# Three projection passes of each attention round moved from slots 12, 14 and 19 to slots 23, 24 and 25

## The reference

```python
proj = n @ w_in[l]                                   # n = RMSNorm(h)
qa, ka, va, qb, kb, vb, gate_a, gate_b = jnp.split(proj, split_at, axis=-1)
o_a = merge(_dilated_attention(qa, ka, heads(va)))   # 8 heads of 64, softmax
o_b = merge(_stick_breaking(qb, kb, vb))             # 8 heads of 64, strictly causal
mixed = (jax.nn.sigmoid(gate_a) * (o_a @ w_up_a[l])
         + jax.nn.sigmoid(gate_b) * (o_b @ w_up_b[l]))
h = h + mixed @ w_out[l]
```

## Time and profile before

| | |
|---|---|
| Median of 3 runs | 1794.56 us (1794.41 to 1795.36) |
| Profiled execution | 1795.2 us, span 1793.3 us |
| TensorE busy | 1709.0 us, 95% of the span |
| VectorE, ScalarE, GpSimd busy | 1145.5, 794.0, 767.5 us |
| TensorE's mean granted clock | 0.991 of full |
| Round 1, first logits (279.88) to those of round 2 (458.21) | 178.3 us |

### The profile page before, as it was taken

The page is one execution under the profiler, slowest core; times in us unless marked ns, Lnnn a source line. Parts: engine busy times, 40 slices in busy tenths (PEclk is TensorE's granted clock), DMA queues, the critical chain, the costliest instruction groups (busy, mean ns, idle before and its releaser), DMA issues.

```text
span 1793.3 us, 24747 instructions
## 1 busy us (share of the span) xinstructions
PE 1709.0 (95%) x8354; PEld 1382.6 (77%) x8354; DVE 1145.5 (64%) x1677; ACT 794.0 (44%) x1304; POOL 767.5 (43%) x876
## 2 busy tenths in 40 slices
PE   5799999999999999999999997999999999999997
PEld 4677777787777777777887875788888888788885
DVE  7536884688468955976644789554554455566665
ACT  6335773577357746863312445443333334100013
POOL 3552322232223221334554334666566566444446
PEclk9899999999999999999999998999999999999999
DMA  5231012102111211245312001222223222422222
GB/s 203 65 118 49 29 54 67 48 29 66 64 39 33 72 56 42 99 157 200 112 47 94 24 24 35 71 71 94 70 70 102 85 70 74 161 94 94 94 94 94
DMA packets 51717, 141.80 MB, mean 79 GB/s; under 512 B 6193, under 2 KB 14641, under 8 KB 51505
## 3 DMA queue, kind: packets, MB, share of 16 engines
q1 hardware_dynamic: 32400, 101.62, 16.4%
q10 hardware_dynamic: 19232, 39.07, 6.7%
HBM read 109.20 MB, written 30.41 MB: 78 GB/s over the span
## 4 chain that ended last, share of the span: by engine, by line
PE 78%; DVE 8%; issue 4%; POOL 2%; ACT 2%; POOLq 0%; DVEq 0%; ACTq 0%
PE ps L569 44%; PE ps L950 22%; PE ps L686 4%; PE ps L649 3%; PE ps L663 3%; DVE e_row L1792 1%; DVE e_row L1789 1%; POOL w_lo L519 1%; DVE rows L1801 1%; DVE pt L1825 1%; DVE sum_a L2019 1%; PE ps L682 1%; PE ps L901 0%; DVE n_lo L2025 0%; PE ps L878 0%
## 5 line engine op out<-in xcount | busy, mean ns | idle before, releaser
L480 POOL TENSOR_SCALAR w_hi<-w_stage 128x512 fp32r<-128x512 f32 x164 | 108.8, 682 | 773.2 <-issue 393.6
L569 PE MATMUL ps<-n_hi,w_hi 128*128 128x512 f32 x1120 | 307.9, 396 | 5.5 <-DVE n_lo L1737 1.9
L485 POOL TENSOR_TENSOR w_lo<-w_stage,w_hi 128x256 fp32r<-128x256 f32 x328 | 301.9, 952 | 6.8
L569 PE MATMUL ps<-n_hi,w_lo 128*128 128x512 f32 x1120 | 303.7, 392 | 0.0
L569 PE MATMUL ps<-n_lo,w_hi 128*128 128x512 f32 x1120 | 303.1, 392 | 0.0
L569 PEld LDWEIGHTS ps<-n_hi,w_hi 128*128 128x128 f32 x1120 | 206.5, 188 | 50.6 <-issue 3.5
L569 PEld LDWEIGHTS ps<-n_lo,w_hi 128*128 128x128 f32 x1120 | 207.9, 188 | 42.6 <-issue 0.2
L569 PEld LDWEIGHTS ps<-n_hi,w_lo 128*128 128x128 f32 x1120 | 207.9, 188 | 42.3
L519 POOL TENSOR_TENSOR w_lo<-w_stage,w_hi 128x256 fp32r<-128x256 f32 x176 | 165.1, 959 | 120.5 <-ACT w_hi L1423 120.2
L1913 DVE TENSOR_TENSOR h<-ps,h 128x512 f32<-128x512 f32 (+1 forms) x176 | 121.3, 690 | 122.3 <-PE ps L569 121.9
L1208 ACT ACTIVATE pt<-ps 128x256 fp32r<-128x256 f32 (+3 forms) x96 | 78.0, 813 | 132.9 <-PE ps L663 132.9
(11 more groups left out here) (260 smaller groups left out, 3179.2 us busy)
## 6 DMA issues: line engine op xcount, KB each, us to landing
w_stage<-weights_in SPq DMA_DIRECT2D x116, 512.0 KB, 3.5
w_stage<-weights_in SPq DMA_DIRECT2D x44, 256.0 KB, 2.9
hidden_scratch<-u_f SPq DMA_DIRECT2D x22, 512.0 KB, 5.4
n_lo<-hidden_scratch SPq DMA_DIRECT2D x22, 512.0 KB, 4.1
gates_scratch<-raw ACTq DMA_DIRECT2D x16, 512.0 KB, 3.0
o_scratch<-o_sum ACTq DMA_DIRECT2D x64, 64.0 KB, 2.2
g_b<-gates_scratch ACTq DMA_DIRECT2D x8, 512.0 KB, 4.2
h<-x_t_in ACTq DMA_DIRECT2D x8, 512.0 KB, 9.2
```

What stands on the lines that cost most here:

```text
L480: ins = pool.tensor_scalar(w_hi[:, b, at], stage[:, b, at], 1.0, 1.0, ALU.mult, ALU.mult)
L485: ins = pool.tensor_tensor(w_lo[:, b, at], stage[:, b, at], w_hi[:, b, at].bitcast(F32), ALU.subtract)
L569: ins = pe.matmul(bank, w[:, b, c:c + P], mv(k), start=(first and n == 0), stop=(last and n == total - 1))
```

## The change

The list of passes per slot of `ROUND` is written anew. The first twelve slots keep their numbers. Before, slots 12 to 27 had 3, 2, 3, 2, 3, 2, 2, 3, 2, 1, 1, 1, 1, 1, 1, 2 passes; now they have 2, 2, 2, 2, 3, 2, 2, 2, 2, 1, 1, 2, 2, 2, 1, 2. The tiles keep their order, so every pass from VA's third on is dealt out one to three places later. `LAST` is as it was.

```diff
 ROUND = Plan(("KB", "QB", "QA", "KA", "VB", "VA", "G0", "G1", "G2", "G3"),
-             [3] * 6 + [2] * 6 + [3, 2, 3, 2, 3, 2, 2, 3, 2] + [1] * 6 + [2], {"TB": (12, 14), "TA": (18, 20)})
+             [3] * 6 + [2] * 6 + [2, 2, 2, 2, 3, 2, 2, 2, 2, 1, 1, 2, 2, 2, 1, 2], {"TB": (12, 14), "TA": (18, 20)})
```

## The result

| | before | after |
|---|---|---|
| Median | 1794.96 us (1794.41 to 1795.68, 4 runs) | 1806.63 us (1804.02 to 1809.54, 4 runs) |
| Profiled execution, span | 1795.2, 1793.3 us | 1804.02, 1802.2 us |
| Round 0, first logits to first logits | 178.83 us | 181.56 us |
| Round 1 | 178.33 us | 180.33 us |
| Round 2 | 176.45 us | 180.98 us |

The change is slower by 11.7 us; the ratio to before is 1.0067, 95% interval 1.0051 to 1.0083. The forecast was 1807.5 us, range 1801 to 1813. The profiled execution is the fastest of the four and 2.6 us under their median, so the traces explain +8.8 us of the 11.7. Rounds 0 to 2 are 9.3 us longer, and the rest of the execution 0.5 us shorter.

What follows compares the result with a forecast made beforehand. TensorE and VectorE were taken to be in balance in slots 12 to 22, TensorE to set the tail. Tail 4.0 + 4.0 + 3.4, removals 3 x 0.3, clock 0.8: +13.1 us on 1794.56, say 1807.5; range 1801 to 1813 us.

Steps and rivals of the forecast that it cites:

- The removals give nothing: Slots 12, 14 and 19: passes taken out become TensorE waits or lateness, with no gain.
- Slot 14's wait: Ahead of slot 14's `attend`: TensorE's wait grows from 0.91 to 2.84 us, taking up slot 12's removed pass.
- the net of slots 12 to 22 is +0.3 us a round: Slots 12 to 22: the three removals together cost +0.3 us a round, bounds -1.3 and +1.0.
- the lateness of slot 16's `attend`: Slot 16: a later `pt` starts `attend` at about 390.5 instead of 390.06; TensorE carries 0.4 us to slot 19's logits.
- fall beside other VectorE work: Slots 12 to 22: reads and GpSimd's weight splits at new times; if they fall badly, +1.0 us a round.
- The tail: Slots 23 to 25: three added passes cost 5.7 us less waits behind them: +4.0, +4.0, +3.4 us in rounds 0 to 2.
- The clock: Low granted clock behind longer waits, mattering in slot 16 and round 2's slot 23: half a stretch, +0.8 us.
- rival 3: Low clock behind each new wait, slot 16 in three rounds and round 2's slot 23: +6.3 us, 1813 us; chance 0.14.
- That the waits are filled (1): VectorE is not the bound; slots 12, 14 and 19 shorten by 5.7 us a round: 1789.5 us; chance 0.05.
- That slot 19's wait goes away (2): VectorE's 1.60 us wait for chunk 19's softplus vanishes: -1.3 instead of +0.3 each round, 1802 us; chance 0.12.
- That nothing comes of it (4): Whole kernel: the work is the same and the time stays at 1794.6 us; chance 0.04.
- The sum: Whole kernel: 4.0 + 4.0 + 3.4 + 3 x 0.3 + 0.8 = +13.1 us, about 1807.5 us.

Runs made afterwards that it cites:

- The experiment without the nine passes: Kernel before with one projection pass left out in each of slots 12, 14 and 19 of rounds 0 to 2: 1795.56 us against 1795.22.
- The read moved by itself: Kernel before with only VectorE's read of VA's first half moved from slot 13 to slot 14, rounds 0 to 2: 1796.56 us against 1796.05.
- the experiment with nine passes more: Kernel before with one more projection pass in each of slots 23, 24 and 25 of rounds 0 to 2: 1808.51 us against 1795.22.
- no longer of the second: Kernel before with two passes moved, from slots 10 and 11 to 22 and 23 (1795.72 us) or 22 and 24 (1796.54 us), against 1795.93.
- the single moves: Kernel before with one pass moved: slot 12 to 23, 1800.63 us; 14 to 24, 1800.12 us; 19 to 25, 1799.26 us; against 1795.59.

## Why the prediction was right

**The removals give nothing: shown.** The experiment without the nine passes takes the time of before. Slot 14's wait was put at 2.84 us and is 2.70 to 2.71 in all three rounds; slot 22's at about 2 and is 2.1. For slot 16 I had about 2 us: it is 0.83 where the low clock stood behind slot 14's wait, 2.92 where it didn't.

**Slots 12 to 22: mis-sized.** The step "the net of slots 12 to 22 is +0.3 us a round" should have said 0.9, and 1.5 in round 2. Two of its terms were too small.

The first is the lateness of slot 16's `attend`. I had it start 0.4 us later; counted from the scans of chunk 12 it starts 392.94 - 371.39 = 21.55 us on, and before 390.06 - 369.19 = 20.87: 0.7 later. The read moved by itself gives 0.6 of it, so nearly the whole read counts there. From that `attend` to the logits of slot 19 TensorE has no gap that could take it, ScalarE's softplus of chunk 19 waits for those logits, and VectorE's scans of chunk 19 wait for the softplus: they start 421.52 - 371.39 = 50.13 us on, in before 49.44, 0.7 later again. In between VectorE was level with before at the scans of chunk 15, as said (23.99 us on against 23.92), and that gained nothing; a head start of VectorE ends as a wait for the softplus, the new 1.36 us at chunk 17 and the 1.43 at chunk 19.

The second is the weight splits that "fall beside other VectorE work", which I had let pass as a bound only. Before, G3's split ran beside the scans of chunk 19, and that pair took 2.82 us. Now it runs at 426.90 beside those of chunk 20, and the pair at 430.31 takes 3.26 us, where before it took 2.34. These are the rows of before: VectorE's start on chunk 15 and its scans of chunks 19 and 20, and GpSimd's split of G3.

```profile
393.11 1.21 DVE L1789 SCALAR_TENSOR_TENSOR e_row<-rows,e_row 128x1024 f32<-128x1024 f32 x1
...
420.26 2.82 DVE L1792 TENSOR_TENSOR_SCAN e_row<-e_row,stat 128x512 f32<-128x512 f32 x2
...
428.12 2.34 DVE L1792 TENSOR_TENSOR_SCAN e_row<-e_row 128x512 f32<-128x512 f32 x2
```

```profile
417.01 3.81 POOL L485 TENSOR_TENSOR w_lo<-w_stage,w_hi 128x256 fp32r<-128x256 f32 x4
```

The first got 0.36 shorter (2.46), as did the L1789 ahead of it (1.59 to 1.23), and the second 0.92 longer: the last 0.2 us of the 0.9.

Round 2's further 0.6 us goes with a split too, that of G1. Without a low stretch in slot 14 TensorE begins G0 in slot 15 1.44 us earlier after the scans of chunk 12 than in round 1, and GpSimd, which waits for that, begins on G1 1.44 us earlier. Here are GpSimd's start and VectorE's L1789 and scans of chunk 14 in round 1, then the scans of chunk 12 and the same three rows in round 2:

```profile
387.91 2.06 POOL L480 TENSOR_SCALAR w_hi<-w_stage 128x512 fp32r<-128x512 f32 x2 [20.89 <-PE ps L569]
...
387.32 0.94 DVE L1789 SCALAR_TENSOR_TENSOR e_row<-rows,e_row 128x768 f32<-128x768 f32 x1
388.30 2.47 DVE L1792 TENSOR_TENSOR_SCAN e_row<-e_row 128x384 f32<-128x384 f32 x2
```

```profile
551.88 1.23 DVE L1789 SCALAR_TENSOR_TENSOR e_row<-rows,e_row 128x1024 f32<-128x1024 f32 x1 [2.44 <-ACT e_row L1193]
...
566.96 1.39 POOL L480 TENSOR_SCALAR w_hi<-w_stage 128x512 fp32r<-128x512 f32 x2 [19.45 <-PE ps L569]
...
567.80 1.35 DVE L1789 SCALAR_TENSOR_TENSOR e_row<-rows,e_row 128x768 f32<-128x768 f32 x1
569.18 2.72 DVE L1792 TENSOR_TENSOR_SCAN e_row<-e_row 128x384 f32<-128x384 f32 x2
```

The two VectorE rows take 0.41 and 0.25 us longer in round 2, slot 16's `attend` comes that much later, and the scans of chunk 19 start 50.75 us on instead of 50.13. TensorE's 1.44 us and VectorE's 0.65 together also account for slot 16's wait of 2.92 us in place of 0.83. The same kernel with the split at another time is close to a test, but no run moved a split and nothing else; that the splits slow VectorE is argued from these pairs of rows.

**The tail: mechanism right, size off in this execution.** The step gave +4.0, +4.0 and +3.4 us; the trace has 22.30 - 20.36 = 1.9, 22.35 - 21.09 = 1.3 and 22.24 - 19.35 = 2.9. The waits ahead of slots 24 and 25 went away as said. I had left the low clock of slot 23 standing in rounds 0 and 1, and this execution has it in slot 14 of rounds 0 and 1 and slot 22 of round 0 instead, where waits cover it. With it in place, as in the experiment with nine passes more, the tail grows by 3.5 and 3.6. Round 1's 0.81 us ahead of the next round's first logits was also gone; I had not looked at it.

**The clock: the term that varies.** I took +0.8. The four runs' mean granted clocks were 0.990, 0.988, 0.986 and 0.986 for 1804.02, 1805.65, 1809.54 and 1807.61 us, so the time goes with the clock, by up to 5.5 us. The wait of 2.71 us ahead of slot 14 had a low stretch behind it in rounds 0 and 1 and none in round 2. The Trainium skill, page "TensorE: Matmul & The Clock Gate", section "HAM oscillation — how this bites in real kernels", lets each burst behind a wait begin slow (in its own example the waits are longer than any here); by these three rounds it does so in two of three, and in both it cost nothing that the trace shows, as another wait stood behind it. The two places that rival 3 priced, slot 16 and round 2's slot 23, had no low stretch in this execution. That slot 16 can have one, and that it costs there, the run with nine passes left out showed: 1.2 us in its round 0, where I had 1.57. Whether the three executions without a profile had more of them is not shown; their clocks and times would fit.

**The other rivals.** That the waits are filled (1) fell with the nine passes left out. That slot 19's wait goes away (2) fell too: VectorE's wait for the softplus of chunk 19 is 1.43 us in place of 1.60, and another of 1.36 us has come ahead of it. That nothing comes of it (4) is outside the interval.

The sum came to +13.1 us and 11.7 was measured. It hit closer than its parts: the tail too large by 5 us in the profiled execution, the stretch too small by 2.4, and the runs at lower clock making up the rest of the median. That the two errors have opposite signs is luck.

## What to carry to other kernels

A busy share of 95% doesn't say that an engine sets the pace. Where two engines arrive at each hand-over together, work taken from the one becomes its waiting, and work put behind the last hand-over is paid in full: look at which wait a moved instruction lies ahead of, not at which slot has room. A pass fills a wait only if it stands ahead of it, and out of a place where its engine has no other clock to follow; here that was true of one pass (slot 11 to 22, -4.2 us) and no longer of the second.

## What the runs showed of the hardware that wasn't expected

The same wait, 2.7 us long and at the same place of the program, was followed by a stretch at the lower clock level in two rounds of one execution and not in the third; the 1.73 us wait of slot 23 by one in rounds 0 and 1 of before, and by none in rounds 1 and 2 of after. The time of one kernel varies with it: 31 executions of before, beside the single moves, went from 1792.67 us at a mean clock of 0.991 to 1799.61 at 0.985. A low stretch costs what no wait behind it takes up. In slot 23 of before `attend` and transposes were 1.57 us slower, and slot 24's wait shrank by 0.6 (1.23 us in round 2, 0.61 in round 1); behind slot 16's wait it cost 1.2 us; in slot 14 of after nothing shows.

VectorE's running sums take longer where they stand beside GpSimd's weight split: the pair of 128x512 2.34 us without it, 3.26 us with it. The Trainium skill, page "SBUF — State Buffer", section "SBUF: two separate sides", says that GpSimd and VectorE contend on a shared port pair; both traces agree in that the slow scans stand where the split stands. What the contention costs a scan is from the rows here.
